# Two more weight chunks in SBUF, a reordered recurrence, a norm shared out and a gather in column groups, in a two-block fp32 kernel

## The reference

```python
# block 1
m_lat = split(silu(c) @ w_mod + b_mod, 6)
h = modulate(rmsnorm(x, norm1_g), m_lat[0], m_lat[1])      # and the same for 256 context tokens
mix = token_mixers(h_lat, h_ctx, w_in, ...)   # windowed attention, gated delta rule, differential attention, Fourier
x = x + m_lat[2] * (mix @ w_out)
h = modulate(rmsnorm(x, norm2_g), m_lat[3], m_lat[4])
x = x + m_lat[5] * expert_choice_ffn(h, w_router, w_gate, w_up, w_down)   # 16 experts, 32 tokens each, width 2048
x = rmsnorm(x, final_norm_g)
# block 2
u = modulate_2(x, ...); proj = u @ w_in
y_a = (gelu(gr) * rg_lru(conv(xr))) @ w_rnn_out;  y_b = dsa_attention(...) @ w_att_out
x = x + g1 * ((ga * y_a + gb * y_b) @ w_out)
x = x + g2 * hier_moe(modulate_2(x, ...), ...)             # 32 experts, width 512
return rmsnorm_2(x, final_g)
```

## Time and profile before

| | |
|---|---|
| median of 3 runs | 2175.1 us (2173.95 to 2176.38) |
| the profiled execution | 2184.12 us, span 2182.2 us |
| PE busy | 1801.7 us (83%) |
| DVE, ACT, POOL busy | 599.6, 275.2, 96.7 us |
| DMA | 728.93 MB, mean 334 GB/s |
| chain that ended last | PE 57%, DMA 36%, DVE 4% |

### The profile page before, as it was taken

The page is one execution under the profiler, slowest core; times in us unless marked ns, Lnnn a source line. Parts: engine busy times, 40 slices in busy tenths (PEclk is TensorE's granted clock), DMA queues, the critical chain, the costliest instruction groups (busy, mean ns, idle before and its releaser), DMA issues.

```text
span 2182.2 us, 28797 instructions
## 1 busy us (share of the span) xinstructions
PE 1801.7 (83%) x11783; PEld 1004.0 (46%) x11783; DVE 599.6 (27%) x1275; ACT 275.2 (13%) x574; POOL 96.7 (4%) x133
## 2 busy tenths in 40 slices
PE   6999888877566766766657665999999899999998
PEld 3677777632122222222222221888888544444343
DVE  4755663510000000000000001566513321122122
ACT  3223330100000000000000001212520100000001
POOL 1012311000000000000000000000200000000000
PEclk9999999787878778787787777999999999999999
DMA  9622026499999999999999999356247799999995
GB/s 392 255 78 99 2 109 251 176 408 432 430 431 431 429 430 432 434 432 431 431 431 431 430 432 417 142 227 235 101 167 305 308 409 427 428 429 428 428 428 247
DMA packets 52759, 728.93 MB, mean 334 GB/s; under 512 B 5892, under 2 KB 6340, under 8 KB 10564
## 3 DMA queue, kind: packets, MB, share of 16 engines
q1 hardware_dynamic: 50544, 720.66, 79.1%
q10 hardware_dynamic: 2132, 7.10, 0.9%
HBM read 726.66 MB, written 1.08 MB: 333 GB/s over the span
## 4 chain that ended last, share of the span: by engine, by line
PE 57%; DMA 36%; DVE 4%; issue 1%; ACT 1%; POOL 0%; SPq 0%; DVEq 0%; ACTq 0%; POOLq 0%
DMA ring<-in_w_moe 34%; PE psum L858 10%; PE psum L996 7%; PE psum L890 5%; PE psum L581 4%; PE psum L869 3%; PE psum L827 2%; PE psum L1424 2%; PE psum L1433 2%; PE psum L599 2%; PE psum L1148 2%; PE psum L1298 1%; PE psum L1160 1%; PE psum L1717 1%; PE psum L1174 1%
## 5 line engine op out<-in xcount | busy, mean ns | idle before, releaser
L581 PE MATMUL psum<-ring,main 128*32 128x512 f32 x2016 | 303.3, 762 | 149.2 <-DMA ring<-in_w_moe 139.0
L581 PEld LDWEIGHTS psum<-ring,main 128*32 128x32 f32 x2016 | 72.3, 135 | 369.5 <-issue 197.1
L858 PE MATMUL psum<-ring,main 128*64 128x512 f32 x1024 | 225.8, 594 | 0.0
L599 PE MATMUL psum<-ring,main 128*32 128x512 f32 x1016 | 149.5, 736 | 79.1 <-DMA ring<-in_w_moe 78.4
L996 PE MATMUL psum<-main,ring 128*128 128x256 f32 x768 | 168.7, 379 | 0.0
L641 DVE TENSOR_TENSOR main<-main,psum 128x512 f32<-128x512 f32 x16 | 11.0, 688 | 568.9 <-ACT main L659 568.9
L996 PEld LDWEIGHTS psum<-main,ring 128*128 128x128 f32 x768 | 145.1, 190 | 21.3 <-issue 0.5
L858 PEld LDWEIGHTS psum<-ring,main 128*64 128x64 f32 x1024 | 73.1, 137 | 147.7 <-issue 147.7
L566 PE MATMUL psum<-main 128*128 128x32 f32 x512 | 91.4, 351 | 31.1 <-DVE main L631 31.1
L599 PEld LDWEIGHTS psum<-ring,main 128*32 128x32 f32 x1016 | 33.8, 127 | 179.3 <-DMA ring<-in_w_moe 108.4
L566 PEld LDWEIGHTS psum<-main 128*128 128x128 f32 x512 | 89.3, 275 | 46.6 <-DVE main L631 44.7
(11 more groups left out here) (474 smaller groups left out, 2103.2 us busy)
## 6 DMA issues: line engine op xcount, KB each, us to landing
ring<-in_w_moe SPq DMA_DIRECT2D x70, 4096.0 KB, 23.6
ring<-in_w_moe SPq DMA_DIRECT2D x137, 2048.0 KB, 16.1
ring<-in_w_mod SPq DMA_DIRECT2D x36, 1024.0 KB, 7.8
ring<-in_w_in SPq DMA_DIRECT2D x36, 1024.0 KB, 4.9
ring<-in_w_moe SPq DMA_DIRECT2D x13, 1024.0 KB, 13.4
main<-in_w_mod SPq DMA_DIRECT2D x12, 1024.0 KB, 6.8
main<-in_w_moe SPq DMA_DIRECT2D x9, 1024.0 KB, 18.2
ring<-in_w_out SPq DMA_DIRECT2D x8, 1024.0 KB, 5.7
```

Of the source, the lines that this page charges most:

```text
L581: last = mm(psum[32 * j:32 * j + 32, b, :], xg1[:, k, :], w[:, 512 * j:512 * j + 512], start=k == 0, stop=k == KT - 1)
L599: last = mm(psum[q:q + 32, BANK_Y, :], hidT[:, P * (f % 4) + 32 * (f // 4):P * (f % 4) + 32 * (f // 4) + 32], w[:, r, 512 * g:512 * g + 51 ...
L858: last = nc.tensor.matmul(psum[CAP2 * u:CAP2 * u + CAP2, b, :], xg2[:, 4 * h + k, CAP2 * u:CAP2 * u + CAP2], w[u][:, k, :], start=h == 0 a ...
```

## The change

**Places.** `main` grows by two chunks (`kept`), which are free through all of the program. Of the `w_mod` chunks from 8 on, every second pair goes there. Then they take chunks 17 and 18 of block 1's expert 0 (`SPARE1` is 7) and chunks 6 and 7 of block 2's first pair of experts (`SPARE2` is 6). `uw`, `kd`, `o_acc`, `state` and `vnew` are placed anew, so that slots 7 to 11 are free early; the `kd` of each direction's last step, which nobody reads, is left out (t is 3 - d). Some semaphores are joined or share one.

```diff
-SPARE1, SPARE2 = 5, 4
+FIRST_FREED = 7
+SPARE1, SPARE2 = 7, 6
+KEPT = 2
...
+                  [("w_mod", c) for c in range(8, 22)] + [("w_out", 0), ("w_out", 1)] + \
+                  [("w_mod", c) for c in range(22, 24)] + [("w_out", 2), ("w_out", 3)]
...
+            if name == "w_mod" and c >= 8 and c // 2 % 2:
+                return SLOTS + c % 2
...
-                sp.dma_start(slot(s)[:, 0:A[key[0]].shape[2]], A[key[0]][key[1]]).then_inc(loaded[s], 16)
+                sp.dma_start(home(s)[:, 0:A[key[0]].shape[2]], A[key[0]][key[1]]).then_inc(loaded[s], 16)
+                if key == ("w_mod", 23):
+                    free_slots(sp)
+                    for n in (7, 8):
+                        moe1_load(sp, 0, n)
...
+            for n in (17, 18):
+                sp.wait_ge(*banks.full(last_user[("w_mod", 22)]))
+                moe1_load(sp, 0, n, spare=True)
...
+            for d in range(2):
+                sp.wait_ge(*banks.full(("uw", 3, d)))
+            for n in (SLOTS, SLOTS + 1):
+                moe1_load(sp, 0, n, spare=True)
+            sp.wait_ge(mix_ready, 3)
...
+                if key == ("w_rg", 1):
+                    for n in (6, 7):
+                        moe2_load(sp, 0, n, spare=True)
```

```diff
-                 "end": [("ws", 2, 1, 3), ("ws", 3, 0, 3), ("wo", 0, 3), ("so", 2, 1, 3), ("so", 3, 0, 3),
-                         ("wo", 1, 0), ("ws", 3, 1, 2), ("wo", 1, 1), ("so", 3, 1, 2),
-                         ("wo", 1, 2), ("wo", 1, 3)]}
+                 "end": [("ws", 2, 1, 3), ("ws", 3, 0, 3), ("open", 0, EARLY[:2]), ("so", 2, 1, 3), ("so", 3, 0, 3),
+                         ("open", 0, EARLY[2:]), ("ws", 3, 1, 2), ("open", 1, EARLY[:4]), ("so", 3, 1, 2),
+                         ("open", 1, EARLY[4:])]}
...
+                    if (t, lv) == (3, LAST):
+                        project_mix(0, 3, EARLY)
...
+                if (kind, *at) == ("so", 3, 0, 3):
+                    head_squares(1)
+                    gate_heads(1)
+                if (kind, *at) == ("so", 3, 1, 2):
+                    head_squares(0)
+                    gate_heads(0)
+            for t in (1, 0):
+                dve.wait_ge(head_rstd_ready, 4 - t)
```

```diff
+                if t == 0:
+                    act.wait_ge(rstd_ready, 4)
+                    for g in range(2):
+                        cs = slice(512 * g, 512 * g + 512)
+                        act.activation(h2[:, 1, cs], x[:, 1, cs], ACT.Copy, scale=rstat[:, 3:4]).then_inc(x_normed, 1)
...
+            pool.wait_ge(gain_scaled, 1)
+            for g in range(2):
+                cs = slice(512 * g, 512 * g + 512)
+                pool.wait_ge(x_normed, g + 1)
+                V.tensor_tensor(h2[:, 1, cs], h2[:, 1, cs], rows[:, 1, cs], ALU.mult).then_inc(pool_step, 1)
+                pool.wait_ge(pool_step, pool_steps())
+                V.tensor_tensor(h2[:, 1, cs], h2[:, 1, cs], rows[:, 2, cs], ALU.add).then_inc(pool_step, 1)
```

```diff
-            for k in range(KT):
-                for t in range(NT):
-                    mm(o[:, CAP1 * k:CAP1 * k + CAP1], h2[:, t, P * k:P * k + P], onehot[:, t, 0:CAP1], start=t == 0, stop=t == NT - 1)
+            for t in range(NT):
+                for j in range(4):
+                    last = mm(o[32 * j:32 * j + 32, 0:256], onehot[:, t, 0:CAP1], h2[:, t, 256 * j:256 * j + 256], start=t == 0, stop=t == NT - 1)
+            last.then_inc(m_rows, 1)
...
-                last = mm(psum[:, BANK_P, P * t:P * t + P], gated[:, t, :], ident, start=True, stop=True)
+                nc.tensor.transpose(psum[:, BANK_P, P * t:P * t + P], gated[:, t, :], ident)
+            pe.wait_ge(m_rows_sb, e + 1)
+            for c in range(2):
+                last = nc.tensor.transpose(o[:, 256 + P * c:256 + P * c + P], x_rows[:, P * c:P * c + P], ident)
```

265 lines of the change are left out of this document (153 added, 112 removed).

## The result

The changed kernel took 2160.61 us (median of 4 runs, 2156.7 to 2163.39), the kernel before 2174.52 beside it (2173.68 to 2176.38): a ratio of 0.9925, 95% interval 0.9907 to 0.9942. So it is 13.9 us faster, where 23 were forecast; 2160.6 lies inside the range, 8.5 us above the point. The profiled execution took 2163.39 us (span 2161.6), 20.7 less than the profiled one before. Why the profiles differ by 7 us more than the medians is the first question of the experiments. Two executions of the kernel before, timed beside later versions, took 600 to 700 us longer at a granted clock of 0.60 and 0.63, and are left out of every figure.

A forecast was written before the change was run, and what follows sets the result against it. Block 1's expert stage was held by the weight stream at 430 GB/s, its end set by the second chunk's use and chunks in SBUF. Terms of -4.9 + 0.7 - 3.5 - 6.3 - 12.5 + 2 + 1.5 = -23.0 gave 2152 us, range 2143 to 2163.

The forecast's parts named there:

- modulation weights: Modulation products behind 300 us: four places instead of two remove PE's waits and the low clock behind the last, -6.3 us.
- end of the recurrence: Chunk 3's values to the finished heads' turn: output products regrouped, waits filled, DVE's tail shorter, -12.5 us.
- gather: Expert 0 of block 1: gathering its rows and gates takes 4.0 us instead of 7.5, -3.5 us.
- heads to expert 0: Finished heads to expert 0's start: PE +3, DVE -2.5, contention +1, together +1.5 us.
- two chunks: Block 1's expert stream: 19 chunks in SBUF instead of 17, -4.9 us, with +0.7 for a longer queue wait.
- the +2 for the lower clock: End of the recurrence: PE still has two waits and may drop to 1.2 GHz for part, +2 us.
- Rival 1: Recurrence stays at the lower clock, costing 8 us more than counted, 6 beyond the allowance: 2158 us, chance 0.15.
- Contention: Finished heads to expert 0: three meetings of DVE and GpSimd operations, +1 us; by the exclusive lock, 5.
- What moves the second use forward moves the end: Block 1's experts: bringing the second chunk's use forward brings the stage's end forward by as much.
- Rival 2: Clock stays up through the recurrence and returns sooner at expert 0, 2 + 2 us: 2148 us, chance 0.12.
- Rival 3: Mixers' gain hidden, above all by DVE; half of 12.5 and of 6.3 lost: 2161.5 us, chance 0.11.
- Rivals 4 and 5: Two chunks don't pay, 2157 us, chance 0.05; stream runs dry in every expert, 2190 us, chance 0.03.

The follow-up runs named there:

- second pair: Second profiles of the kernel before and the changed kernel, neither edited: 2175.28 and 2158.95 us, a difference of 16.3.
- first pair: First profiles of the kernel before and the changed kernel, as shown: 2184.1 and 2163.39 us, a difference of 20.7.
- two places: Changed kernel with two places for the modulation weights instead of four: median 2166.5 us, ratio 0.9949 to the kernel before.
- the other edit: Changed kernel with the residual products of the output projection's last two groups put earlier: median 2155.6 us, ratio 0.9902 to the kernel before.
- output products ahead: Changed kernel with the recurrence end's first two output products put ahead of the first state products: median 2155.9 us, ratio 0.9919 to the kernel before.

## Why the prediction was right, and where not

The direction, the mechanism and the sign of every term were right, but the change brought some 14 to 17 us of the 23, and the range of 2143 to 2163 holds it only near its upper end. The sum divides so; against the differences of the profiles, 16.3 and 20.7 us, the columns leave out what lies ahead of 300 us (0.6 more in the second pair, 0.9 less in the first):

| step | forecast | second pair | first pair |
|---|---|---|---|
| modulation weights, 300 to first output product | -6.3 | -4.4 | -7.3 |
| end of the recurrence | -12.5 + 2 | -6.3 | -6.6 |
| gather, heads to expert 0, two chunks: router's load to last expert product | -3.5 + 1.5 - 4.9 + 0.7 = -6.2 | -5.1 | -5.4 |
| behind the last expert product | 0 | -1.0 | -0.5 |

*Modulation weights.* The waits went, and DVE was late next, as said: PE waits 1.53 us behind the last of these products. The step that failed is "the low clock behind that wait also goes: 1.6". It went, but it had not been there in every execution. Of the four profiles with these waits (the kernel before twice, with the new gather alone, and two places) two have it and a first stage of 53.6 to 53.8 us, two have not and stand at 50.6 and 50.7. The term was right for the execution of the earlier trace rows and is up to 1.6 too large for one without it. In the sum, 5.7 less 0.9 is 4.8 and not 4.7.

*End of the recurrence.* The new order did what was counted, and from the last value product to the heads' turn it took 4.1 us, with 4.0 forecast. What was mis-sized is the +2 for the lower clock. These two rows of the changed kernel, six products in twelve records, stand at 1.2 GHz where I priced them at 2.4 (1.0 and 1.9 us), and the value products, 2.00 before, take 3.68:

```profile
375.67 2.07 PE L1751 MATMUL psum<-ring,main 128*128 128x256 f32 x4
377.68 0.70 PE L1731 MATMUL psum<-ring 128*64 128x64 f32 x8
378.30 3.68 PE L1735 MATMUL psum<-ring 128*128 128x64 f32 x16
381.77 3.73 PE L1751 MATMUL psum<-ring,main 128*128 128x256 f32 x8
```

That is 1.1 + 1.7 + 1.8 = 4.6 us. Rival 1 had named it, with 8 us and a chance of 0.15; the truth lies between it and the forecast. The wait of 0.70 us ahead was in the prediction's count, with the +2 for its clock; in the one profile with the output products put into it, most of the loss is gone.

*Heads to expert 0 and the gather.* The gather took 2.5 us instead of 4.0: it ran at the higher clock. So did the first products of the experts behind it, 1.7 us less, which the prediction had at nothing; the old gather put back cost 3.7 + 1.6 = 5.3, against the 3.5 of the forecast. The rest of the way was forecast at +1.5 and came at +5.2 in the first pair (from 31.0, 410.74 to 441.78, to 36.2, 396.09 to 432.31) and at +6.7 in the second (29.6 to 36.2). In the second pair no step was sized worse. Of it 0.8 and 2.3 lie ahead of DVE's first routing operation, and 4.5 from there to its last of the norm (11.5 to 16.0); 2.5 of these are contention, the rest is work of DVE that stands elsewhere in the order now, the gain's scaling (1.23) among it. Two things were too small. The output products that moved in here, priced at +3 less 2.5 for DVE's lighter load, hold DVE's last addition, and putting them elsewhere gave 4.1 back, 1.7 of them by the clock. Contention, priced at +1 from the earlier trace rows, was 2.5 us on DVE; avoiding it gave 1.2 by itself, where the scan was caught instead, and 2.5 on top of the other edit, where four operations had been caught. The rows show one operation behind another rather than side by side: DVE's operation of 128x16 began at 419.49 and ended at 420.41, just after GpSimd's of 418.74 ended at 420.37. The Trainium skill (SBUF — State Buffer, "SBUF: two separate sides") describes the shared port pair as an exclusive lock held for a whole instruction; the trace agrees for these forms. By it I had put the contention at up to 5, and by the rows at 1; 2.5 lies between, and that the page's sum of +5.5 is close to the measured +5.2 is luck: the other half of the +5.2 is not contention. For the search's operations, 0.42 and 0.40 with GpSimd beside them and without, the trace shows no such cost.

*Two chunks.* -4.2 in all was forecast and 4.0 measured by taking them away.

*What moves the second use forward moves the end.* Right in the changed kernel, in every version that moved it. Wrong for the kernel before: there, by the version with the new gather alone, only 2.2 of 5.9 us passed. The prediction had 2.5 idle us of the DMA engines ahead of the use from the one profile, and the second one has hardly any (0.99 in both stretches of 10 us from 440 to 460). The edits depend on each other: by this count it is the six more chunks ahead of the router's load (ten, before four) that give the later edits their worth; no version took them away alone. The prediction's 35 us from the heads' turn to the second use, for the transfers that remain, should be 40 by its own marks (394 to 434), which changes nothing.

*Rivals.* Rival 2 (the clock stays up) came half true: not in the recurrence, where "output products ahead" shows that it nearly can, but at expert 0, where the granted clock was 1.00 through the gather and the first products, some 3 us better than counted (1.5 + 1.7). Rival 3 came out nearest in time, 2161.5, but its mechanism was only part of it: of DVE's share 2.5 us. Rivals 4 and 5 are out: the two chunks pay, and the experts' stage ran at 430 GB/s.

*What would show it.* Heads' turn near 394 (396.1 and 394.5), gather at 4 us (2.5), second use near 434 (436.8 and 435.2), last expert product near 1327 (1329.7 and 1327.9), block 2 as before (831.9 and 829.3). Each came within 3 us. One sign of being wrong did come up: the second chunk's use should come forward by 12 us at least. It did by 16.2 in the first pair, but only by 9.5 in the second (444.71 to 435.20), since the kernel before had reached it 8.3 us sooner than in its first profile. The mark had been set by that one execution. Of the 8.5 us between the forecast and the median, 6.7 are the difference between 23.0 and the second pair's 16.3; the rest is within what medians of these few runs differ by (13.9 us between them the first time, 17.0 the second).

## What to carry to other kernels

Before a term is read from a low-clock row, look whether a second execution has it; a price that stands on one execution's bad luck can't be subtracted from the median. The same holds for an experiment: 1.7 of the 2.9 us that moving GpSimd's passes seemed to give were such a draw, found only by dividing the stage at the first operation that the edit could reach. Where a stream of weights bounds a stage, ask not when the consumer is ready but whether the DMA engines stand idle ahead of it: time saved there is worth at most that idle time, and the same edit gave 2 us with the engines full and 5 with them idle. And when a low stretch stands in the way, fill the wait ahead of it and look: it helped where 3.16 us were filled, in three profiles of three, and where 0.70 us were, in one, while dividing the products within the stretch helped nothing.

## What the runs showed of the hardware

- A DVE operation of 128x16 that takes 0.23 us alone took 0.92 and 1.00 beside a GpSimd pass of 128x512 (1.26 alone), and a scan of 16x256 went from 0.68 to 1.71. A maximum or a match over 16x256 was not touched (0.42 and 0.40), nor was a reciprocal of 128x1 (0.16). GpSimd pays too: its operation of 128x1 took 1.00 instead of 0.19 where it met DVE's of 128x1024.
- A fall to 1.2 GHz in the recurrence recurred in the profiles of the changed kernel's order (granted 0.50 from about 372 to 385 us in the second one), and the stage with it had the same length, 47.8 us, in seven of nine. Four records of PE work, moved into a wait of 0.70 us, took 3.8 to 5.4 us off it, in one profile. The clock fell there too, but later and for a shorter time. Why so short a wait should decide, or whether it does, was not settled.
- Behind a wait of 3.16 us of PE, 28 records of 128x256 took 7.7 to 7.9 us in seven of eight profiles (granted 0.78 in the second profile of the changed kernel) and 6.21 in one; behind a wait of 0.57 us they took 6.21 in three of three (1.00).
- With no edit between them, executions of the kernel before spread over 15 us, the ten of the changed kernel over 7 (2156.7 to 2163.4). Part of the spread is in block 2, whose time moved between 827.6 and 832.4 us.
